# One visit of TensorE for a scan's outputs, the next round's logits and key norms, and a layer norm's variance

## The reference

```python
r, k, v, g, dw, da = split(token_shift(pa, mu))
log_w = -softplus(-(w0 + tanh(dw) @ w2)) - 0.5      # logits, w2 is 64 x 1024
a = sigmoid(a0 + da @ a2)                           # logits, a2 is 64 x 1024
kk = k * k_k
kh = kk / max(sqrt(sum(kk * kk over a head)), 1e-12)  # key norm, heads of 64
# a scan over time with decay, k, v, kh, a gives y
yn = (y - mean) * rsqrt(var(y over a head) + 64e-5)   # layer norm of a head
out = (yn * ln_w + ln_b + bonus) * silu(g)
```

## Time and profile before

| what | value |
|---|---|
| runs | 1116.33 us median of 3 (1116.11 to 1116.51) |
| the profiled execution | 1117.01 us, its span 1115.3 us |
| granted TensorE clock, mean | 0.996 of full speed |
| PE busy | 1100.5 us, 99% |
| PE weight loads | 918.8 us, 82% |
| DVE busy | 807.8 us, 72% |
| ACT busy | 610.7 us, 55% |
| POOL busy | 42.5 us, 4% |
| large matmuls of the rounds, L1372 and L1375 | 1424 each |
| split_lo on DVE, L853 | x352, mean 1247 ns |
| split_hi on ACT, L455 | x356, mean 1051 ns |

### The profile page before, as it was taken

One profiled execution on the slowest core, in us unless ns is written; L12 is line 12 of the kernel. 1 busy time (PEld: TensorE's weight loads), 2 busy tenths in 40 slices (PEclk: granted clock), 3 DMA queues, 4 the chain that ended last, 5 costly groups with the idle time before them and its releaser, 6 DMA issues.

```text
span 1115.3 us, 22920 instructions
## 1 busy us (share of the span) xinstructions
PE 1100.5 (99%) x8006; PEld 918.8 (82%) x8006; DVE 807.8 (72%) x1257; ACT 610.7 (55%) x934; POOL 42.5 (4%) x68
## 2 busy tenths in 40 slices
PE   7999999999999999999999999999999999999997
PEld 5888888888888888888888888888888888888885
DVE  6888889798897988889888858445555555556564
ACT  6666575665756657576475645445344544435443
POOL 2000000000000000000000120000000000000000
PEclk8999999999999999999999999999999999999999
DMA  7766656556475655656556565666666576667663
GB/s 200 206 162 181 171 141 171 157 160 167 129 189 148 180 152 141 183 144 176 143 164 176 153 189 156 222 207 189 191 191 196 158 226 200 195 179 270 212 192 109
DMA packets 254556, 197.24 MB, mean 177 GB/s; under 512 B 23111, under 2 KB 206640, under 8 KB 254128
## 3 DMA queue, kind: packets, MB, share of 16 engines
q1 hardware_dynamic: 251748, 195.81, 60.6%
q10 hardware_dynamic: 2764, 0.85, 0.3%
HBM read 193.71 MB, written 2.11 MB: 176 GB/s over the span
## 4 chain that ended last, share of the span: by engine, by line
PE 98%; DVE 1%; ACT 1%; ACTq 0%; issue 0%
PE ps L1372 31%; PE ps L1375 15%; PE ps L1473 12%; PE ps L1475 12%; PE ps L1474 12%; PE ps L1761 3%; PE ps L1762 3%; PE ps L1760 3%; PE ps L1507 1%; PE ps L1685 1%; PE ps L1546 0%; PE ps L1402 0%; PE ps L1645 0%; PE ps L1709 0%; PE ps L1554 0%; PE ps L1582 0%
## 5 line engine op out<-in xcount | busy, mean ns | idle before, releaser
L853 DVE TENSOR_TENSOR wlo<-raw,whi 128x1024 fp32r<-128x1024 f32 x352 | 434.3, 1247 | 218.4 <-ACT whi L455 216.6
L1372 PE MATMUL ps<-hx,whi 128*128 128x512 f32 x1424 | 516.2, 405 | 1.4 <-DVE hx L884 1.3
L455 ACT ACTIVATE whi<-raw 128x1024 fp32r<-128x1024 f32 (+1 forms) x356 | 370.3, 1051 | 252.8 <-PE ps L1475 182.4
L1375 PE MATMUL ps<-hx,wlo 128*128 128x256 f32 x1424 | 399.6, 281 | 0.0
L1372 PEld LDWEIGHTS ps<-hx,whi 128*128 128x128 f32 x1424 | 268.0, 188 | 69.1 <-issue 6.9
L1375 PEld LDWEIGHTS ps<-hx,wlo 128*128 128x128 f32 x1424 | 269.8, 189 | 1.1 <-DVE lots L893 0.5
L1473 PE MATMUL ps<-whi,hx 128*128 128x512 f32 x384 | 150.4, 392 | 0.0
L1475 PE MATMUL ps<-whi,hx 128*128 128x512 f32 x384 | 149.6, 390 | 0.0
L1474 PE MATMUL ps<-wlo,hx 128*128 128x512 f32 x384 | 149.5, 389 | 0.0
L1475 PEld LDWEIGHTS ps<-whi,hx 128*128 128x128 f32 x384 | 72.1, 188 | 15.0
L1473 PEld LDWEIGHTS ps<-whi,hx 128*128 128x128 f32 x384 | 72.1, 188 | 14.9 <-issue 0.2
(11 more groups left out here) (285 smaller groups left out, 1048.4 us busy)
## 6 DMA issues: line engine op xcount, KB each, us to landing
raw<-in_w_in SPq DMA_DIRECT2D x548, 256.0 KB, 3.2
raw<-in_w_branch SPq DMA_DIRECT2D x96, 256.0 KB, 3.7
raw<-in_w_out SPq DMA_DIRECT2D x64, 256.0 KB, 3.7
o<-in_x SPq DMA_DIRECT2D x4, 512.0 KB, 5.6
o<-in_x SPq DMA_DIRECT2D x2, 1024.0 KB, 8.7
acb<-acs_rows SPq DMA_DIRECT2D x7, 256.0 KB, 3.4
out_y<-lots SPq DMA_DIRECT2D x5, 256.0 KB, 2.5
lots<-in_final_norm_w SPq DMA_DIRECT2D x1, 1024.0 KB, 11.5
```

The costliest lines, as they stand in the source:

```text
L455: sc.activation(whi[:, slot, :, 0:width], raw[:, slot, :, 0:width], ACT.Copy).then_inc(hi_done, 1)
L853: tt(wlo[:, slot, :, :], raw[:, slot, :, :], whi[:, slot, :, :].bitcast(F32), ALU.subtract).then_inc(lo_done, 1)
L1372: mm(ps[:, bank, :], whi[:, slot, k, wcol], hx[:, kt].rearrange("p a t -> p (a t)"), start=first, stop=False, skip_group_check=True)
L1375: return mm(ps[:, bank, 0:T], wlo[:, slot, k, wcol], hhi[:, kt, :], start=False, stop=last, skip_group_check=True)
```

## The change

- **One visit.** V_VAR is 33. The visit behind slot 28 goes. Behind slot 33 PE now runs the SSD outputs first, then norm_and_logits(j + 1), then the variance. Key norm and variance are one fp32 matmul each of 128x128 by 256 columns. The wait ahead of it is for ysq_ok and kk_sq; var_rt and ob_d are waited for no more, lora_lo in the visit is new.
- **Logits.** The low-rank weights and their input are split: lrs holds the input's high half and, in the other 64 partitions, its low half; lorat is loaded twice, into both halves of the partitions (four DMAs in place of two), ACT copies it to lorah (slot 13), GpSimd subtracts to loral. Each logit is two single-pass matmuls of 128 rows by 256 columns. SP loads them at the round's start behind the second strip, no more behind the fourth.
- **DVE's order.** The SSD operations go from slot 29 to 34. The variance's reciprocal goes from slot 32 to 36, the rest of the layer norm from 34 to 38, so both stand behind kk_recip and decays (slot 35). kk_floor is one instruction. In slots 10 and 12 the solve stands ahead of the slot's split_lo.
- **ACT's order.** The variance's square root goes from slot 29 to 35, behind kk_root, as one instruction. half_logits waits for ob_d as well.
- Semaphores of the row norms and of dt are merged.

```diff
-V_VAR = V_ST + NC
+V_VAR = 33
             def load_lora(j):
-                sp.dma_start(lorat[0:64, 0, :], rw_w2[0, :, bass.ds(j * P, P)]).then_inc(lora_in, 16)
-                sp.dma_start(lorat[64:128, 1, :], rw_a2[0, :, bass.ds(j * P, P)]).then_inc(lora_in, 16)
+                for w, src in enumerate((rw_w2, rw_a2)):
+                    for h in range(2):
+                        sp.dma_start(lorat[side(h), w, :], src[0, :, bass.ds(j * P, P)]).then_inc(lora_in, 16)
...
+            def lora_split_lo(j):
+                pool.wait_ge(s["lora_hi"], j + 1)
+                gp.tensor_tensor(loral[:], lorat[:], lorah[:].bitcast(F32), ALU.subtract).then_inc(s["lora_lo"], 1)
...
+            def lora_split_hi(j):
+                act.wait_ge(lora_in, j * 64 + 64)
+                sc.activation(lorah[:], lorat[:], ACT.Copy).then_inc(s["lora_hi"], 1)
...
-                    if t == V_VAR + 1:
+                    if t == 35 and not last:
+                        kk_root(j + 1)
+                    if t == 35:
                         act.wait_ge(s["var_mm"], j + 1)
-                        sc.activation(nrm[:, 0:P], C[:, 0:P], ACT.Sqrt, scale=1.0 / 64, bias=eps3[:, 1:2])
-                        for e in range(2):
-                            op = sc.activation(nrm[side(e), P:T], B[side(1 - e), P:T], ACT.Sqrt, scale=1.0 / 64,
-                                               bias=eps3[side(e), 1:2])
-                        op.then_inc(s["var_rt"], 1)
+                        sc.activation(nrm, A[:, T:2 * T], ACT.Sqrt, scale=1.0 / 64, bias=eps3[:, 1:2]).then_inc(s["var_rt"], 1)
...
                     if t == 35 and not last:
-                        kk_root(j + 1)
+                        act.wait_ge(s["ob_d"], j + 1)
                         half_logits(j + 1)
...
-            def norm_and_logits(j, bank):
-                for h in range(2):
-                    for e in range(2):
-                        op = mm(ps[side(e ^ h), bank if h else 5, h * T:h * T + P], head1[side(e), side(e)],
-                                ksq[side(e), h * P:h * P + P], start=True, stop=True)
-                op.then_inc(s["kk_mm"], 1)
-                pe.wait_ge(lora_in, j * 32 + 32)
-                mm(A[:, 0:T], lorat[0:64, 0, :], lr[0:64, :], start=True, stop=True)
-                mm(C[:, 0:T], lorat[64:128, 1, :], lr[64:128, :], start=True, stop=True).then_inc(s["lora_mm"], 1)
+            def norm_and_logits(j):
+                pe.wait_ge(s["lora_lo"], j + 1)
+                for w, dst in enumerate((A[:, 0:T], C[:, 0:T])):
+                    mm(dst, lorah[:, w, :], lrs[:, w, :], start=True, stop=False)
+                    op = mm(dst, loral[:, w, :], lrs[:, w, :], start=False, stop=True)
+                op.then_inc(s["lora_mm"], 1)
+                mm(B[:, 0:T], head1[:], ksq, start=True, stop=True).then_inc(s["kk_mm"], 1)
```

More of the change, by code:

```diff
@@ L290, in main @@
                 strip(c + 4, (SC0 + j * P, SC0 + W + j * P))
+                if not last:
+                    sp.wait_ge(s["lora_mm"], j + 1)
+                    load_lora(j + 1)
                 cols = (SC0 + 2 * W + j * P, SC0 + 3 * W + j * P)
@@ L407, in main @@
                 if not last:
+                    lora_split_lo(j + 1)
                     kk_unit(j + 1)
+            lora_split_lo(0)
             pool.wait_ge(s["sc_mm"], NG)
@@ L643, in main @@
                         low(strip0, 1, BANKS[0], zp[:, 0, :])
+                    if t == 13 and not last:
+                        lora_split_hi(j + 1)
                     if t == 17:
@@ L1058, in main @@
                 for t in range(2 * (LAST + GATES) if last else SLOTS):
+                    if t == 10:
+                        for k in range(5, 8):
+                            solve_step(k)
+                        solve_corner(8)
+                    if t == 12:
+                        solve_corner(9)
+                        dve.wait_ge(s["sol_r"], j * 9 + 9)
+                        v.tensor_copy(sol_l, sol_t.rearrange("p s t -> p t s")).then_inc(s["sol_tr"], 1)
                     if t % 2 == 0 and t // 2 < nchunks and t not in (V_ST, V_ST + 2):
@@ L1218, in main @@
                         fold_shift(j + 1, 0, BANKS[3] + 1)
-                    if t == 32:
+                    if t == 33 and not last:
+                        shift(j + 1, 0)
+                        kk_floor(j + 1)
+                    if t == 34:
+                        dve.wait_ge(s["yb_mm"], j + 1)
+                        dve.wait_ge(s["sc_f"], j + 1)
+                        stt(cv, xs2, dskh[:, bass.ds(j, 1)], E[:, T:2 * T], ALU.mult, ALU.add).then_inc(s["ob_d"], 1)
+                        dve.wait_ge(s["ob_d"], j + 1)
+                        dve.wait_ge(s["z2_ok"], j + 1)
+                        stt(o[:, 1, bass.ds(j, 1), :], cv.unsqueeze(1), 0.5, zp[:, 1:2, :], ALU.mult, ALU.mult
+                            ).then_inc(s["ob_ok"], 1)
+                    if t == 35 and not last:
+                        kk_recip(j + 1)
+                        decays(j + 1)
+                    if t == 36:
                         dve.wait_ge(s["var_rt"], j + 1)
                         v.reciprocal(rin, nrm).then_inc(s["ln_v"], 1)
-                    if t == 33 and not last:
-                        shift(j + 1, 0)
-                        kk_floor(j + 1, 7)
-                    if t == 34:
+                    if t == 38:
                         dve.wait_ge(s["ln_v"], j * 3 + 1)
@@ L1233, in main @@
                             ).then_inc(s["oa_ok"], 1)
-                    if t == 35 and not last:
-                        kk_recip(j + 1)
-                        decays(j + 1)
             with dve.Fori(0, CT - 1) as j:
@@ L1569, in main @@
                         half_chunk(base + c, c % RING, c % 4, t % 2, BANKS[a], lambda: ready_behind(t))
-                    if t == 33 and not last:
-                        norm_and_logits(j + 1, 7)
                     if t == 4:
@@ L1695, in main @@
                     if t == V_VAR:
-                        if last:
-                            pe.wait_ge(s["ysq_ok"], j + 1)
-                        for h in range(2):
-                            for e in range(2):
-                                op = mm(ps[side(e ^ h), 6 - h, h * P:h * P + P], head1[side(e), side(e)],
-                                        ysq[side(e), h * P:h * P + P], start=True, stop=True)
-                        op.then_inc(s["var_mm"], 1)
                         pe.wait_ge(s["xst_ok"], j + 1)
@@ L1712, in main @@
                         op.then_inc(s["yb_mm"], 1)
+                        if last:
+                            pe.wait_ge(s["ysq_ok"], j + 1)
+                        else:
+                            norm_and_logits(j + 1)
+                        mm(A[:, T:2 * T], head1[:], ysq, start=True, stop=True).then_inc(s["var_mm"], 1)
             with pe.Fori(0, CT - 1) as j:
```

76 lines of the change are left out of this document (31 added, 45 removed).

## The result

| what | before | after |
|---|---|---|
| runs, median | 1116.11 us (1115.53 to 1116.51, 5) | 1136.95 us (1136.72 to 1137.50, 5) |
| ratio | | 1.0189, 95% interval 1.0178 to 1.0200 |
| span of the profiled execution | 1115.3 us | 1135.7 us |
| granted TensorE clock, mean | 0.996 | 0.994 |
| first to last round's score matmuls (7 rounds) | 108.2 to 585.7, 477.5 us | 108.7 to 606.3, 497.6 us |

A forecast was written before the change was run, and what follows sets the result against it. PE, always busy, was taken as the bound, so only small-matmul cost and PE's waits count. Against 1117.0 us: -1.9 - 0.2 + 9.1 + 9.3 = +16.3, 1133.3, less 0.7 for the runs' median: 1133, range 1120 to 1142.

The forecast's parts named there:

- PE's own work: PE's small-matmul visits: merged visit 2.33 us against 2.58 for two, 0.25 saved a round; -1.9 us in sum.
- the four independent 64x64 tiles: Rule against the saving: the four variance matmuls would cost one 128-column pass, about 0.22; saving nearly gone.
- Slot 4: PE waits for the shift behind DVE's longer queue: 1.3 us a round, 9.1 in seven rounds.
- Rival E: split_lo slowed beside GpSimd, both stretches of waits at their long ends: +25.2, 1141.5 us; chance 0.08.
- n_in and tb: SP's loads around the solve: n_in 1.9 us later, DVE waits 0.5; tb issued 1.75 later, lands 1.8 later.
- Slots 14 to 19: PE waits at slots 16, 18, 19 for split_lo, tx, p1: 0.2, 0.7, 0.4 us; 9.3 in all.
- Rival B: Only slot 4 waits, as n_in and tb land in time: +7.0, 1123.3 us; chance 0.17.
- C: DVE's queue is short enough, only PE's work counts: -2.1, 1114.2 us, if DVE's chain ends before 245.1; chance 0.08.
- D: No difference: waits of about 0.3 us a round against the 0.28 saved, 1116.3 us; chance 0.05.

The follow-up runs named there:

- the kernel with both parts back: Changed kernel with the four lora loads back behind the fourth strip and the solve back behind split_lo: 1122.65 us, 1.0061 of before.
- the kernel with the two DVE edits and both parts back: Changed kernel, lora loads and solve back, variance's reciprocal ahead of decays, SSD operations ahead of kk_floor: 1112.62 us, 0.9975 of before, the fastest measured.
- the two kernels with one edit alone: Kernel before the change plus only the solve ahead of split_lo: 1122.80 us; or plus only the four early lora loads: 1120.12 us.

## Why the prediction was right, and where it was off

The forecast was 1133 with a range of 1120 to 1142; the time is 1136.95. The mechanism was right in all of its parts, the size 4 us short.

- **PE's own work.** Forecast visit 2.33, measured 2.33. The row of the fp32 matmuls held too: 234.14 - 233.71 = 0.43, as in the earlier trace rows. So the saving is the 0.25 a round that the rows gave. By the four independent 64x64 tiles of the Trainium skill (TensorEngine Tiling (Array Packing), Tiling Modes) it would have been nearly gone; the four quarter-array matmuls take 0.38, not half of 0.43, and by the measurement the saving is there.
- **Slot 4, forecast 1.3 a round, measured 1.36 (9.5 in all, forecast 9.1).** From the start of the visit (232.24) the steps came out like this: kk_floor's input 2.10 (forecast 2.13), the split_lo behind decays 8.02 (8.08), the end of the shift 19.09 (18.93). The split_lo behind decays took 1.36 beside the end of GpSimd's second multiply, where I had taken 1.14; these 0.22 are more than the 0.16 by which the shift is late. Rival E had a wait of 1.9 from this slowing; of its 0.6 a round, 0.2 came. (E was itself too low: the three split_lo of the earlier trace rows lost 4.51 - 3.42 = 1.09, and with all of that kept the wait is 2.4.)
- **n_in and tb.** Forecast 1.9 later, 0.5 wait, tb issued 1.75 later and landed 1.8 later; measured 2.0, 0.62, 1.9 and 1.9. Reading SP's queue was enough for this.
- **Slots 14 to 19, forecast 9.3 in all, measured 12.7: the term that was mis-sized.** Two things were missing. First, the instants at which PE wants slots 16, 18 and 19 were taken from the third round, which runs at the slower of two paces (below). In four rounds of seven of the kernel before PE gets to slot 18 another 0.37 earlier, and what it gains there it waits: 1.5 us. Second, the first round: there SP's two loads of the second lora matrix took 2.20 us to issue, where they take 1.19 in the third, n_in came another 1.0 later, and PE stood at slot 14; that round cost 1.2 more than the others at its pace. The rest is that the forecast's 1.3 is 1.4 to 1.5 in the rounds for which it was worked out (the third, fifth and seventh). Why one issue took so long in the first round stays open. Slot 14, whose split_lo the solve of slot 10 is now ahead of, costs 0.2 in most of the other rounds and was not foreseen either. It adds nothing to a round's sum: the third round has no such wait and costs 1.5, the fifth and seventh have it and cost 1.4, as PE then waits less at slot 18.

The first round, SP, then DVE, then PE:

```profile
110.52 2.20 SPq L268 DMA_DIRECT2D lorat<-in_rw_a  x2
```

```profile
118.01 0.15 DVE L1054 TENSOR_TENSOR lots<-lots 32x2 f32<-32x2 f32 x1 [1.73 <-DMA lots<-ad]
```

```profile
124.30 0.50 PE L1392 MATMUL ps<-hx,whi 128*128 128x512 f32 x1 [0.96 <-DVE wlo L872]
```

- **Rival B** (n_in and tb land in time) falls by the kernel with both parts back: at slots 14 to 19 lie 14.3 us. **C** (only PE's work counts) had the right condition: it describes the kernel with the two DVE edits and both parts back, at 1112.6 us where C said 1114.2. D falls with the two groups of waits, which are ten times what it allows.

## What to carry to other kernels

When PE is busy all the time, the work between two of its small visits is a deadline problem on the other engines: merging visits saved PE 0.25 us a round, and moving work between the key norms and the shift on DVE cost 1.4, until the same work was put where DVE waits for something else. Look at the brackets in the queue that is late: a queue can be the bound and still hold idle time, and an independent instruction belongs ahead of the one that waits. On a queue that only issues transfers, a prefetch that nobody waits for goes behind the transfer that somebody waits for: the same four loads cost some 5 us on one side of n_in and nothing on the other.

## What the runs showed that I had not expected

PE runs the same pair at two paces, 0.347 and 0.353 us, at a granted clock of 1.00 in both. Where no wait comes between, it holds one of them from slot 4's visit to slot 18's. Two rounds of the kernel before, each from the first to the 56th large 512-column matmul between slot 4's visit and slot 18's, the second round and the third:

```profile
178.19 0.47 PE L1372 MATMUL ps<-hx,whi 128*128 128x512 f32 x1
...
197.34 0.39 PE L1372 MATMUL ps<-hx,whi 128*128 128x512 f32 x1
```

```profile
246.25 0.48 PE L1372 MATMUL ps<-hx,whi 128*128 128x512 f32 x1
...
265.76 0.40 PE L1372 MATMUL ps<-hx,whi 128*128 128x512 f32 x1
```

19.15 against 19.51 us for 55 pairs, the first of which is some 0.08 longer than the others in both. The clock of stretches of the same rounds (start and end, length, busy time and instructions of PE, PEld, DVE, ACT, POOL, granted clock, DMA share, GB/s):

```profile
178.00:197.00 19.00, 19.00 (x113) 16.64 (x112) 17.17 (x34) 12.69 (x22) 0.00 (x0) 1.00 0.62 160
...
246.00:265.00 19.00, 19.00 (x110) 16.53 (x110) 17.15 (x34) 12.56 (x22) 0.00 (x0) 1.00 0.62 161
```

In the kept execution of the kernel before, this stretch is slow in the third, fifth and seventh rounds and fast in the others; in the fastest kernel's it is fast in all of them, and 3 x 0.37 = 1.1 us of the 3.8 between the two spans (1115.3 and 1111.5) come from that. Slots 29 to 32 too go from the slower to the faster pace where the visit behind slot 28 is gone, in every round, 0.1 us each. So not all of the 3.8 is work that the merged visit saved, which was 1.75. The slower rounds between slots 4 and 18 may belong to the execution and not to the kernel: it took 1117.01 us, above the kernel's medians of 1115.5 to 1116.1, the two kernels with one edit alone have no such round in their traces, and there is one trace of each. What sets the pace was not tried, and stays open. It has a practical side: a margin read in one round, as mine was at slot 18, is only good for that pace.
